# Expert weight tiles of a mixture-of-experts stage loaded in pairs

## What is computed

```python
h = silu(einsum('td,edf->tef', xf, w_gate)) * einsum('td,edf->tef', xf, w_up)
y = einsum('tef,te,efd->td', h, gate, w_down)      # e: 16 experts, d: 2048, f: 512
x = layer_norm(ALPHA * x + y, ln2_g, ln2_b)
```

## Time and profile before

| what | us |
|---|---|
| median of three runs | 1497.19 (1496.46 to 1498.79) |
| the profiled execution | 1493.46 |
| its span, from the first to the last instruction | 1491.6 |
| TensorE busy, whole span | 1439.3 (96%) |
| VectorE, ScalarE, GpSimd busy | 1015.0, 770.8, 190.4 |
| before the experts' stage | about 0 to 820 |
| blocks in the loop | about 870 to 1406 |
| last block, last down parts and final norm | about 1406 to 1491.6 |

### The profile page before, as it was taken

The page is one execution under the profiler, slowest core; times in us unless marked ns, Lnnn a source line. Parts: engine busy times, 40 slices in busy tenths (PEclk is TensorE's granted clock), DMA queues, the critical chain, the costliest instruction groups (busy, mean ns, idle before and its releaser), DMA issues.

```text
span 1491.6 us, 24267 instructions
## 1 busy us (share of the span) xinstructions
PE 1439.3 (96%) x9396; PEld 1291.7 (87%) x9396; DVE 1015.0 (68%) x1287; ACT 770.8 (52%) x912; POOL 190.4 (13%) x99
## 2 busy tenths in 40 slices
PE   8999999999999999999997999999999999999995
PEld 7999999999999999999996467888888888888772
DVE  4246746757777787523125668888888888888877
ACT  4245545444434433411110047777777777777774
POOL 0000000000000000234330001121121211222130
PEclk9999999999999999999998899999999999999998
DMA  7321231322213312633435699999999999999997
GB/s 262 123 89 57 86 114 61 96 90 86 88 57 115 116 58 73 205 111 146 145 96 205 207 394 375 384 401 391 392 375 384 384 382 398 387 390 401 348 294 232
DMA packets 74389, 335.36 MB, mean 225 GB/s; under 512 B 12086, under 2 KB 18790, under 8 KB 45514
## 3 DMA queue, kind: packets, MB, share of 16 engines
q1 hardware_dynamic: 68842, 315.54, 56.2%
q0 software_dynamic: 5472, 18.74, 5.0%
HBM read 313.56 MB, written 40.73 MB: 238 GB/s over the span
## 4 chain that ended last, share of the span: by engine, by line
PE 85%; DVE 7%; DMA 3%; ACT 2%; issue 2%; POOL 0%; ACTq 0%; SPq 0%; DVEq 0%; POOLq 0%
PE BANK L1811 13%; PE BANK L1812 13%; PE BANK L1813 13%; PE BANK L2170 7%; PE BANK L2172 7%; PE BANK L2171 7%; PE BANK L2222 4%; PE BANK L2220 4%; PE BANK L2221 4%; PE BANK L2154 2%; DMA RAWB<-in_w_up 2%; PE BANK L2183 2%; PE BANK L1953 1%; PE BANK L1829 1%; PE BANK L2050 1%
## 5 line engine op out<-in xcount | busy, mean ns | idle before, releaser
L1811 PE MATMUL BANK<-XH,HI 128*128 128x260 f32 x1746 | 503.0, 288 | 1.4 <-DVE RT L1487 1.0
L1683 DVE TENSOR_TENSOR LOB<-RAWB,HIB 128x2048 fp32r<-128x2048 f32 x196 | 448.6, 2291 | 74.0 <-ACT HIB L1050 73.1
L1812 PE MATMUL BANK<-XL,HI 128*128 128x260 f32 x1746 | 495.3, 284 | 0.0
L1813 PE MATMUL BANK<-XH,LO 128*128 128x260 f32 x1746 | 494.3, 283 | 0.0
L1050 ACT ACTIVATE HIB<-RAWB 128x2048 fp32r<-128x2048 f32 x196 | 376.4, 1921 | 86.0 <-PE BANK L2172 66.1
L1811 PEld LDWEIGHTS BANK<-XH,HI 128*128 128x128 f32 x1746 | 331.2, 190 | 2.7 <-issue 1.7
L1812 PEld LDWEIGHTS BANK<-XL,HI 128*128 128x128 f32 x1746 | 331.1, 190 | 0.7
L1813 PEld LDWEIGHTS BANK<-XH,LO 128*128 128x128 f32 x1746 | 330.9, 190 | 0.0
L2170 PE MATMUL BANK<-HIB,XGH 128*128 128x512 f32 x512 | 201.8, 394 | 5.5 <-issue 3.0
L2172 PE MATMUL BANK<-LOB,XGH 128*128 128x512 f32 x512 | 200.0, 391 | 0.0
L2171 PE MATMUL BANK<-HIB,XGL 128*128 128x512 f32 x512 | 199.8, 390 | 0.0
(11 more groups left out here) (388 smaller groups left out, 1674.5 us busy)
## 6 DMA issues: line engine op xcount, KB each, us to landing
RAWB<-in_w_down SPq DMA_DIRECT2D x68, 1024.0 KB, 9.5
RAWB<-in_w_gate SPq DMA_DIRECT2D x67, 1024.0 KB, 9.4
RAWB<-in_w_up SPq DMA_DIRECT2D x67, 1024.0 KB, 8.9
RAW<-in_w_in SPq DMA_DIRECT2D x39, 1024.0 KB, 4.9
RAW<-in_w_out SPq DMA_DIRECT2D x16, 1024.0 KB, 5.0
Y<-in_xT SPq DMA_DIRECT2D x8, 520.0 KB, 9.1
RT<-in_xT SPq DMA_DIRECT2D x16, 260.0 KB, 5.2
x_rows<-R SPq DMA_DIRECT2D x5, 832.0 KB
```

The source lines that it names most:

```text
L1683: dve.tensor_tensor(LOB[:, s, :], RAWB[:, r, :], HIB[:, s, :].bitcast(F32), ALU.subtract).then_inc(b_lo[s], 1)
L1811: pe.matmul(bank, hw[:, c, :], h, start=(c == 0), stop=False)
L1812: pe.matmul(bank, hw[:, c, :], l, start=False, stop=False)
L1813: ins = pe.matmul(bank, lw[:, c, :], h, start=False, stop=(c == KC - 1))
```

## The change

Loads of two neighbouring tiles are one transfer of 2 MB into two neighbouring slots. Its issue waits for both slots and it counts once, on the semaphore of the even slot. For this the gate and up tiles are ordered gate, gate, up, up, so that a pair is 16 KB contiguous in a partition; TensorE's bank and chunk numbers follow. A down pair is four rows of 1024 values a partition, as its two tiles were. Block 0's loads stay single. The column tiles of the last two down parts stay single transfers, but both wait for both slots. In block 1 `x1_out` moves behind pair (0, 1), `y_set(0)` and `(1)` stand before pair (4, 5), `(2)` and `(3)` before pair (6, 7), and `(4)` behind it. The shared helper `bload` keeps only block 0's case. `bhi` takes an optional count (`landed`), used for tiles 9 and 11 of the last block and 1 and 3 behind it.

```diff
@@ -588,18 +588,25 @@
-            def bload(i, m0, w, j):
+            def bload(i, w):
 
                 s = i % NRAW
-                if m0 is None:
-                    sp.dma_start(first_tile(i), w).then_inc(b_raw[s] if i < NRAW else s_wr, 16)
-                    return
-                if isinstance(j, int) and i < NRAW:
-                    sp.wait_ge(b_used, i + 1)
+                sp.dma_start(first_tile(i), w).then_inc(b_raw[s] if i < NRAW else s_wr, 16)
+
+            def pair_in(i, w, j, columns=None):
+
+                s = i % NRAW
+                for t in (i, i + 1):
+                    if isinstance(j, int) and t < NRAW:
+                        sp.wait_ge(b_used, t + 1)
+                    else:
+                        sp.wait_ge(b_lo[(2 + t) % NHL], (2 + t) // NHL + 1 + 4 * (j - 1))
+                        passed(sp)
+                if columns:
+                    for t in range(2):
+                        sp.dma_start(RAWB[:, s + t, :].rearrange("p (c n) -> p c n", c=4), columns[t]).then_inc(b_raw[s + t], 16)
                 else:
-                    sp.wait_ge(b_lo[(2 + i) % NHL], (2 + i) // NHL + 1 + 4 * (j - 1))
-                    passed(sp)
-                sp.dma_start(RAWB[:, s, :], w).then_inc(b_raw[s], 16)
+                    sp.dma_start(RAWB[:, s:s + 2, :].rearrange(w[1], **w[2]), w[0]).then_inc(b_raw[s], 16)
...
             def gate_up(j, m0):
                 e = sp.value_load(EBI[0:1, bass.ds(j, 1)], min_val=0, max_val=NE - 1)
-                for i in range(8):
-                    if isinstance(j, int) and i == 1:
+                for i in range(0, 8, 2):
+                    if isinstance(j, int) and i == 2:
                         x1_out(3)
                         x1_out(4)
-                    if isinstance(j, int) and 3 <= i < 3 + NT:
+                    if isinstance(j, int) and i >= 4:
+                        y_set(i - 4)
                         y_set(i - 3)
-                    bload(i, m0, (a["w_gate"], a["w_up"])[i % 2][bass.ds(e, 1), :, 2048 * (i // 2):2048 * (i // 2) + 2048].rearrange("a p n -> p (a n)"), j)
+                    half = 4096 * (i // 4)
+                    w = (a["w_gate"], a["w_up"])[i // 2 % 2][bass.ds(e, 1), :, half:half + 4096].rearrange("a p n -> p (a n)")
+                    pair_in(i, (w, "p s n -> p (s n)", {}), j)
+                if isinstance(j, int):
+                    y_set(4)
 
             def down(j, first, columns=False):
                 e = sp.value_load(EBI[0:1, bass.ds(j - 1, 1)], min_val=0, max_val=NE - 1)
-                for n in range(4):
+                for n in range(0, 4, 2):
+                    w = a["w_down"][bass.ds(e, 1), :, :, 512 * n:512 * n + 1024]
                     if columns:
-                        w, parts = a["w_down"][bass.ds(e, 1), :, :, 512 * n:512 * n + 512].rearrange("a p c n -> p (a c) n"), 4
+                        pair_in(first + n, None, j, [a["w_down"][bass.ds(e, 1), :, :, 512 * x:512 * x + 512].rearrange("a p c n -> p (a c) n") for x in (n, n + 1)])
                     else:
-                        w, parts = a["w_down"][bass.ds(e, 1), :, 2 * (n % 2):2 * (n % 2) + 2, 1024 * (n // 2):1024 * (n // 2) + 1024].rearrange("a p c n -> p (a c) n"), 1
-                    i = first + n
-                    s = i % NRAW
-                    sp.wait_ge(b_lo[(2 + i) % NHL], (2 + i) // NHL + 1 + 4 * (j - 1))
-                    passed(sp)
-                    sp.dma_start(RAWB[:, s, :].rearrange("p (c n) -> p c n", c=parts), w).then_inc(b_raw[s], 16)
+                        pair_in(first + n, (w.rearrange("a p c n -> p (a c) n"), "p s (c n) -> p (s c) n", {"c": 2}), j)
...
-            def bhi(i, m0, j):
+            def bhi(i, m0, j, landed=None):
                 s, r = (2 + i) % NHL, i % NRAW
-                act.wait_ge(b_raw[r], 16 * (2 + i // NRAW) + 32 * (j - 1))
+                if landed:
+                    act.wait_ge(b_raw[r], landed)
+                else:
+                    act.wait_ge(b_raw[r - r % 2], 16 * (2 + i // NRAW) + 32 * (j - 1))
...
                 for i in range(8):
                     hw, lw = ready(i, m0, j)
-                    b = BANK[:, i % 2, :]
+                    b = BANK[:, i // 2 % 2, :]
                     for c in range(4):
-                        cc = 4 * (i // 2) + c
+                        cc = 8 * (i // 4) + 4 * (i % 2) + c
```

More of the change, by code:

```diff
@@ L639, in _ @@
                     sp.wait_ge(s_ob, 2 * KC)
-                bload(i, None, (a["w_gate"], a["w_up"])[i % 2][0, :, 2048 * (i // 2):2048 * (i // 2) + 2048], 0)
+                bload(i, (a["w_gate"], a["w_up"])[i % 2][0, :, 2048 * (i // 2):2048 * (i // 2) + 2048])
             sp.wait_ge(s_rcp, 5 * NT)
@@ L1119, in _ @@
                         bhi(i, 0, j + 1)
-            for i in range(7, 10):
+            for i in range(7, 9):
                 bhi(i, 0, last)
+            bhi(9, 0, last, 32)
             silu(last)
@@ L1125, in _ @@
             column_copy(0, 8, last)
-            bhi(11, 0, last)
+            bhi(11, 0, last, 32)
             column_copy(1, 9, last)
@@ L1130, in _ @@
             column_copy(2, 10, last)
-            bhi(1, 0, nb)
+            bhi(1, 0, nb, 32)
             column_copy(3, 11, last)
@@ L1134, in _ @@
             column_copy(0, 0, nb, YO2, LAST_DOWN_BANK)
-            bhi(3, 0, nb)
+            bhi(3, 0, nb, 48)
             for n in range(1, 3):
```

## The result

| | before | after |
|---|---|---|
| median of the runs compared | 1497.99 us (1496.46 to 1501.92) | 1537.06 us (1533.27 to 1540.39) |
| ratio, with its 95% interval | | 1.0256 (1.0224 to 1.0288) |
| the profiled execution | 1493.46 us | 1540.39 us |
| its span, mean clock | 1491.6 us, 0.982 | 1538.5 us, 0.975 |

The change costs 39 us. The forecast was 1517, the range ended at 1528: the direction and the place were right, and the size was half of what came. Between the two profiled executions the span grew by 46.9, and this is the number that the traces can split. Some 8 of it are the choice of executions: the one of before lies 4.5 under its median, the one of after 3.3 over its own.

What follows compares the result with a forecast made beforehand. TensorE was taken to bound the expert blocks, busy 480.0 of 480.0 us. Waits of 15.4 + 2.6 + 1.7 = 19.7 us over the profiled 1493.46 gave 1513.2; with the median 3.7 higher, forecast 1517, range 1499 to 1528.

Steps and rivals of the forecast that it cites:

- the wait at tile 8: TensorE's waits at the first down tile for pair (8, 9), summed over fourteen blocks: 15.4 us.
- the room that was given them: Gate and up pairs land before use: (6, 7) 2.4 us after tile 9's old issue, wanted at 3.6; no wait.
- 7.5 for a pair: Latency of a 2 MB transfer: 5.0 us for one tile plus 2.5 for one more MB.
- Rival C: A pair behaves as two transfers that don't overlap: 10.0 us each, total 1549; chance 0.04.
- The condition T + 10.4: T is pair (8, 9)'s issue; tile 8 may land up to 10.4 us later before TensorE waits.
- The latency 7.5 + a: Pair (8, 9)'s landing after issue; a is what the scatter into y_rows takes from the queue, 1.8 to 5.7 us.
- the 2.6 of pair (10, 11): TensorE's waits for the second down pair in three blocks: 0.6 + 0.8 + 1.2 = 2.6 us.
- The three b above 1.4: Pair (10, 11) lands 5.0 + b behind (8, 9); after a wait there, TensorE waits b - 1.4 us.
- rival B: Each wait also costs TensorE's clock, some 1.7 us; ten waits, 17 more: 1534; chance 0.06.
- The start: Block 1, full queue: pair (8, 9) lands at 898.9, tile 8 is split at 903.2, formerly started at 901.56: 1.7 us.
- The end of the stage: Column tiles stay single, the first of each two issued one tile later: cost 0, at worst 2.5 us.
- Rivals A and D: A: not measurably slower, queue stays full, 1499.6, chance 0.12. D: faster through longer rows, 1496, chance 0.04.

## Why the prediction was half right

The mechanism was the right one, and the time was wrong for two terms of the sum: the clock, put at nothing, came to 13.4 us in the loop, and the wait at tile 8, put at 15.4, came to 24.0.

**What bounds the kernel, and where it would hurt: right.** TensorE's waits sit at the down tiles, behind `w_down` copies of ScalarE. No gate or up tile in the loop waited for its split, as pairs (0, 1) to (6, 7) had the room that was given them.

**7.5 for a pair: right in a short queue, not at (8, 9).** Gate and up pairs into a short queue land 7.1 to 7.5 after their issue (the `w_up` pair issued at 1147.2: 7.1). Rival C, 10.0 for every pair, falls. But the prediction used 7.5 for (8, 9) without the scatter, and there the kernel without scattered rows has 7.9 to 10.2. The condition T + 10.4 held: at 9.5 to 9.9 tile 8 had no wait, at 10.8 one of 0.35 us, from 12.6 on always one of over 2.

**The latency 7.5 + a: the mechanism right, the size wrong.** In the eight heavy blocks the prediction's terms give 10.5 to 13.2 us and the pair took 12.6 to 14.2. The block near T = 1041 has the largest miss: 0.1 us of wait predicted, 3.76 measured. In sum the 15.4 of tile 8 became 24.0, and even that flatters it, as 2.0 of the 15.4 were foreseen in three light blocks, where no such wait came.

Which half of the sum failed, the kernel without scattered rows tells as far as it can. The a of the eight heavy blocks add up to 36.6; the latencies of after less those without rows, to 37.1. So in sum a was right, by luck, since the single values are off by up to 2.3 either way. The latencies without rows are 0.7 to 2.7 over 7.5 in these blocks, 11.7 together, and that is nearly the whole miss of 12.2. So the best reading is that 7.5 was too low for a pair in a queue that other loads and the gather share. It stays a reading, as that kernel has no waits in the loop and may meet a fuller queue.

Another explanation would be that the tile of before landed in the middle of the scatter, so that its latency held only a part of the scatter's price. GpSimd's next step waits for the scatter's landing and dates it, for the fourth T in before and in after:

```profile
1037.85 0.24 POOL L763 COPY YIXC<-YIX 128x1 int32 x1 [4.30 <-DMA y_rows<-YO,YIXC]
```

```profile
1051.79 0.18 POOL L772 COPY YIXC<-YIX 128x1 int32 x1 [4.42 <-DMA y_rows<-YO,YIXC]
```

In before the scatter landed at 1037.85 and tile 9 at 1036.4; in all eight heavy blocks tile 9 landed within 1.4 us of the scatter's end, on either side. In after the pair landed 1.2 to 3.7 us behind the scatter (here 1055.5 and 1051.79). So most of the scatter was over when the tile of before landed, and this explanation holds at most for a small part. What made the pair of the fourth block land 3.7 us behind its scatter stays open.

Of the 2.6 of pair (10, 11) only 0.4 came, in one of the three blocks (a wait at 1209.26). The three b above 1.4 (2.0, 2.2 and 2.6) stand in the blocks with gathers of 97, 120 and 128 rows, two of them with light scatters, so they look like the gather's price rather than the scatter's. With the waits at the turns of tokens (0.9), the waits in the loop are 25.3 where 18.0 were predicted.

A bound was at hand: the number of rows per block splits the fourteen blocks in two groups with one between, and it could have told the gather's part from the scatter's.

**The clock: wrong.** It stood as rival B, at 0.06, against a window in which 2.10 of 4 us busy had left the clock at 1.00. The trace of after, the window behind the wait of 2.53 us that ended at 943.07, then those at and behind the wait of 3.76:

```profile
942.00:952.00 10.00, 8.93 (x43) 7.52 (x44) 9.98 (x8) 7.94 (x8) 0.00 (x0) 1.00 1.02 429
...
1060.00:1062.00 2.00, 2.00 (x7) 1.62 (x8) 2.00 (x2) 1.65 (x2) 0.00 (x0) 0.74 0.94 401
1062.00:1064.00 2.00, 2.00 (x7) 1.54 (x6) 2.00 (x4) 0.54 (x1) 0.00 (x0) 0.50 0.64 156
```

0.50 is the lower level, 1.2 of 2.4 GHz. The steps with waits of up to 2.53 us kept clock 1.00 and lost at most 0.2 beyond their waits; the six with 2.66 to 3.76 lost 1.8 to 2.9 each, 12.5 of the 13.4. The prediction took its one pause without a fall as a rule for all, and its waits, at most 2.8, were shorter than those that came. Rival B had the price nearly right (1.7 per wait, measured 2.1 on average) and was wrong on how many: six, not ten.

**The start: half.** Tile 6 was to start at 895.7 and started at 897.03, since pair (6, 7) landed at 892.7 (891.4 predicted) and pair (8, 9) at 900.7 (898.9). The clock adds to it: the first matmuls behind the pause of 4.41 us take 0.63 us where they take 0.39 later.

```profile
897.03 0.75 PE L2183 MATMUL BANK<-HIB,XGH 128*128 128x512 f32 x1 [4.41 <-DVE LOB L1696]
...
898.42 0.63 PE L2183 MATMUL BANK<-HIB,XGH 128*128 128x512 f32 x1
...
903.50 0.39 PE L2183 MATMUL BANK<-HIB,XGH 128*128 128x512 f32 x1
```

3.6 us in place of 1.7. Not all of it is the pairs': by its profiled execution the order alone brings 1.6 of it. The kernel without scattered rows has the start as its only wait (5.4 us) and is 5.1 above the median of before.

**The end of the stage: nearly.** 0 was taken and 2.5 kept as the worst; TensorE waited 1.05 for a column tile.

**The sum.** Predicted 15.4 + 2.6 + 1.7 = 19.7. Measured between the profiled executions: waits in the loop 25.3, clock in the loop 13.4, start 3.6, behind the exit 4.8, less 0.2 in the last step: 46.9. Of the 27 us missed between these executions (20 by the medians), about 13 are the clock in the loop, 7 the waits, 2 the start and 5 what lies behind the exit.

**Rivals A and D** were refuted by the DMA share (0.94 where A wanted 1.01) and by the result.

## What to carry to other kernels

Two transfers joined under one count make the consumer of the first half wait for the second half and for all that lands beside it; ask for each consumer how late its own bytes may come, at the place where another stream meets the queue. The price of such a meeting can't be read off a transfer of another size at another place in the queue: count what each stream carries, here the rows of scatter and gather, which differ by block, and let the transfer's own time in that queue have a range. And where a tight loop gets waits of some 3 us for the first time, put TensorE's clock into the sum, not into a rival.

## What the runs showed of the hardware

**The same pause costs clock in one execution and not in another.** At the loop's exit TensorE idles 2.97 us in before and in after, for the same reason. The 4 us behind it, before (clock 1.00), after (0.69), and the kernel with the order alone (0.60, behind 3.01 us):

```profile
1410.00:1414.00 4.00, 4.00 (x18) 3.29 (x19) 2.73 (x2) 1.04 (x1) 0.00 (x0) 1.00 0.94 365
```

```profile
1452.00:1456.00 4.00, 3.98 (x12) 3.24 (x13) 2.61 (x2) 0.00 (x0) 0.00 (x0) 0.69 0.95 352
```

```profile
1414.00:1418.00 4.00, 4.00 (x11) 3.19 (x12) 2.67 (x2) 0.00 (x0) 0.00 (x0) 0.60 0.81 283
```

18 matmuls against 12 and 11, 1.6 us by the time to the next wait (20.56 us in before, 22.2 in the others). The length of one pause doesn't decide alone; what does, these runs don't show. The Trainium skill, "TensorE: Matmul & The Clock Gate", Part 1, says that the monitor runs freely against the kernel, so that the same kernel has a different number of slow matmuls at its start from run to run. These traces are in line with it, with 18 and 12 matmuls in the 4 us behind the same 2.97 us, though they are of two kernels and not of two runs of one.

**A scatter (here one that adds to memory) slows the queue while it keeps it full.** After again, 4 us beside pair (8, 9) in the block with a scatter of 63 rows and a gather of 22, then in one with a scatter of 25 and a gather of 72, then 4 us with neither. Last, the same stretch of the fourth block in the kernel without scattered rows, where the gather of 22 rows is left:

```profile
1045.00:1049.00 4.00, 4.00 (x19) 3.32 (x18) 3.52 (x2) 3.26 (x2) 2.38 (x1) 1.00 1.04 265
1121.00:1125.00 4.00, 4.00 (x19) 3.30 (x18) 3.52 (x2) 3.26 (x2) 2.25 (x1) 1.00 1.02 343
...
1240.00:1244.00 4.00, 2.60 (x7) 2.09 (x8) 4.00 (x3) 3.02 (x4) 0.00 (x0) 0.73 1.07 444
```

```profile
1038.40:1042.40 4.00, 4.00 (x19) 3.31 (x18) 3.40 (x2) 3.30 (x2) 2.53 (x2) 1.00 1.03 375
```

The share is 1.02 to 1.07 in all; the rate is 265, 343, 444 and 375 GB/s. A full queue is no measure of how fast loads land. That the adding is what slows it, and not the writing of rows as such, no run shows. The latency of pair (8, 9) with the rows, less that without, was -0.4 to 1.6 us at 22 to 29 rows, 1.0 at 43, and 3.6 to 5.5 from 63 to 128: no line through the rows, as 63 rows cost 5.3 and 128 rows 4.0. Why, was not settled.
